# The second 512 columns of four output projections by Strassen's scheme, and the order of the adds behind the experts

## The chip, the cores and the metric

One core of a Trainium2 chip runs the whole program in one launch. The metric is the time on the device in microseconds (us); lower is better. The kernel before takes 2987.09 us, the median of 3 runs from 2985.12 to 2989.6.

TensorE (PE) multiplies and transposes. It reads SBUF and writes PSUM, which has 8 banks, each 512 float32 values wide on each of 128 partitions. VectorE (DVE), ScalarE (ACT) and GpSimd (POOL) do the rest; SyncE (SP) issues most DMAs. The engines run side by side and meet only at semaphores.

## The reference

Two blocks run one after the other on x, which is 512 tokens by 1024 features in float32. The first block has two layers, each a mixer and then a layer of 32 experts. The second block has two layers of this form, and all of it is float32:

```
u = rms_norm(h, mix_pre_g)                       # layer 0 dilated, layer 1 differential attention
y = attention(u, w_in, positions) @ w_out        # output projection 1 and 3
h = h + rms_norm(y, mix_post_g)
u = rms_norm(h, mem_pre_g)
y = memory_cross_attention(u, mem, wq, wkv) @ wo # output projection 2 and 4
h = h + rms_norm(y, mem_post_g)
u = rms_norm(h, ffn_pre_g)
h = h + rms_norm((silu(u @ w_gate) * (u @ w_up)) @ w_down, ffn_post_g)
```

An output projection is a 512x1024 by 1024x1024 product. The norm behind it needs a whole row of y, so both halves of the columns.

## The kernel before

**Data.** x stays in SBUF as four tiles of 128 tokens (`x_res`). The input of every projection lies transposed in `ring_feat` (`featv`, eight chunks of 128 features by 512 tokens). Weights come in pieces of 1024x512 through two ring slots, also part of `ring_feat`. A piece is loaded as soon as the piece two before it has been used.

**Output projections** (`out_projection`, line 2634). Half 0 makes columns 0 to 511, half 1 columns 512 to 1023. Each half takes the four token tiles in turn. A tile is eight products of 128x128 by 128x512, one for each chunk of features; each float32 product stands in the trace as two records. ACT squares a bank (L2609), DVE multiplies the same bank by the gain (L2613). After the second half of a tile, POOL takes the root of the mean square (L309, L311), DVE adds the scaled y to x (L2595), ACT squares and scales x for the next norm (L316, L324), with another root on POOL between them. PE transposes the scaled tile (L334) and DVE copies it to `featv` with the gain (L341). This runs one tile behind the products: tiles 0, 1 and 2 are transposed inside half 1, tile 3 inside the next stage. That stage is `memory_queries` (L2677) or `gate_up` (L2987). Each begins with four products of tokens 0 to 255 alone, and finishes them for tokens 256 to 511.

In three of the four projections PE begins half 0 early, while the attention still runs (`out_begin`, `out_products`, L2630). The differential attention leaves one of eight chunks for the end, the memory attention two. Only the dilated attention leaves all of them.

**Strassen's scheme** is already used for the query, gate, mix and down projections. The four blocks of each factor give seven block products in place of eight (Winograd's form). DVE forms four sums and four differences of blocks, each of 128x1024 (L2389 to L2404), before the products that read them. A group of seven products covers two token tiles of a 512-column piece. ACT then copies three products out of PSUM, DVE adds four times, POOL three times. In `down_projection` the last slot makes two such groups. Its outputs go through `down_outputs`, whose order of work is written by hand for each engine, and a layer's last tiles enter the next layer's norm from there.

**Behind the experts** (`combine`, `entry_norm`). For each token tile DVE adds two rows that were read back from DRAM (L1842, L1846). ACT squares tile 0, POOL takes its root, and ACT scales it only after it has squared tile 1. DVE waits for the root of tile 0 (`n_root`) before it adds tile 1. POOL also makes one spare power, at L1826, when the last expert rows have been stored.

Of the kernel before, what the change touches and what calls it, by code (L numbers as in the profile page):

```python
# [5 lines left out]
P = 128  # L6
D = 1024
S = 512
TT = S // P
# [67 lines left out]
def program(nc, a):  # L77
# [5 lines left out]
    with ctx:  # L83
# [265 lines left out]
        def entry_norm(name, eng, buf, gain, added=None, add=None):  # L349
# [3 lines left out]
            if name == "dve" and add:  # L353
                add(0)
                eng.wait_ge(n_root, j + 1)
# [5 lines left out]
            for t in range(TT):  # L361
# [8 lines left out]
                if name == "pool":  # L370
                    root_x(eng, j + t)
# [1436 lines left out]
        def spilled(name, eng, l):  # L1808
# [13 lines left out]
            if name == "pool":  # L1822
# [3 lines left out]
                G.tensor_tensor(out=stat[:, 254:255], in0=c_("ones")[:, 0:1], in1=stat[:, 255:256], op=ALU.pow)  # L1826
# [534 lines left out]
        STAGES = ("mix", "query", "gate", "down")  # L2361
        FAST = {"mix": 10, "query": 2, "gate": FC - 2, "down": 4}
        UP_FULL, SILU = {k: 7 for k in STAGES}, {"mix": 3, "query": 3, "gate": 5, "down": 5}
        HIDDEN, ADDED = {"mix": 4, "query": 4, "gate": 6, "down": 4}, {k: 3 for k in STAGES}
        SUMS = {"mix": 6, "query": 2, "gate": FC // 2, "down": DOWN_SLOTS}
# [268 lines left out]
        def out_projection(name, eng, l, post, nxt, attended=False):  # L2634

            buf = view(big, 0 if attended else 8192, TT, D)
# [6 lines left out]
            for half in range(2):  # L2643
                going = bool(begun) and half == 0
                if name != "pe" or not going:
                    n = take(name, "ring")
                    w = ring_slot(n, KC, 512)
                    if name == "pe":
                        eng.wait_ge(w_loaded[n % 2], 16 * (n // 2 + 1))
                for t in range(TT):  # L2650
                    if name == "pe" and going:
                        out_products(eng, t, range(begun["next"][t], KC)).then_inc(bank_full, 1)
                        take(name, "full")
                    elif name == "pe":
                        def job(bank, t=t, w=w):
                            for k in range(KC):
                                yield T.matmul(bank, featv[:, k, t * P:(t + 1) * P], w[:, k, :], start=k == 0, stop=k == KC - 1)  # L2657
                        pe_bank(eng, job, "both")
                        if half:
                            y_squares.append((bank_read_act, total["act"]))  # L2660
# [1001 lines left out]
```

## Time and profile before

| | us |
|---|---|
| median of 3 runs | 2987.09 |
| the profiled execution, its own time | 2987.54 |
| its span, first to last instruction | 2985.7 |
| PE busy | 2830.2 (95%) |
| DVE busy | 1122.7 (38%) |
| ACT busy | 662.0 (22%) |
| POOL busy | 516.5 (17%) |

The mean granted clock of TensorE over the span is 0.984 of full speed. The records of half 1 and the transposes around it are from 1511.7 to 1541.9 us (dilated), 1660.3 to 1690.4 (memory, layer 0), 2392.8 to 2422.9 (differential) and 2542.1 to 2572.2 (memory, layer 1). The adds behind the experts start at 598.13 us and at 1197.75 us.

The views used are the page itself, the timeline (start, duration, engine, line, operation, output and inputs, shape, count, and in brackets the idle time of the engine before it and what ended it), the view of one tile's instructions, and the view by stretches of time.

### The profile page before, as it was taken

How to read it: one execution, taken by the hardware profiler on the slowest of the kernel's cores; microseconds unless marked ns; L12 is line 12 of the kernel's file. 1: busy time of each engine (PE TensorE's matmuls, PEld its weight loads, DVE VectorE, ACT ScalarE, POOL GpSimd, SP SyncE). 2: the span in 40 equal slices, each digit the busy share in tenths (PEclk: the TensorE clock that was granted, in tenths of full speed). 3: DMA queues.
4: the chain of work that ended last, by engine and by line, in shares of the span. 5: the costliest groups of instructions: out<-in, count | busy, mean ns of one | idle time of the engine just before them, and what ended most of it. 6: DMA issues, size and time to landing. Idle time of an engine off the chain costs nothing.

```text
span 2985.7 us, 32062 instructions
## 1 busy us (share of the span) xinstructions
PE 2830.2 (95%) x12340; PEld 1902.8 (64%) x12340; DVE 1122.7 (38%) x2302; ACT 662.0 (22%) x1512; POOL 516.5 (17%) x799
## 2 busy tenths in 40 slices
PE   8999998789999988899999999999998999999998
PEld 4565543245655432586566688888685565688887
DVE  4543311145433110435532333344447632343354
ACT  3333110033331100104512211101205522211100
POOL 3111111131011111113300012201114510122201
PEclk9999999999999998999999999999999999999999
DMA  3106699831066999421011122222220030222222
GB/s 137 68 29 254 255 414 419 356 124 74 29 254 247 413 419 363 180 86 56 29 57 57 57 85 86 97 79 92 85 85 29 1 113 29 85 85 85 71 80 90
DMA packets 126415, 422.07 MB, mean 141 GB/s; under 512 B 10480, under 2 KB 14704, under 8 KB 103088
## 3 DMA queue, kind: packets, MB, share of 16 engines
q1 hardware_dynamic: 112944, 387.01, 34.0%
q0 software_dynamic: 12736, 30.84, 2.8%
q8 instruction: 101, 1.65, 0.2%
q10 hardware_dynamic: 576, 2.10, 0.2%
q14 instruction: 58, 0.48, 0.1%
HBM read 408.63 MB, written 27.26 MB: 146 GB/s over the span
## 4 chain that ended last, share of the span: by engine, by line
PE 74%; issue 9%; DMA 9%; DVE 3%; ACT 2%; POOL 1%; POOLq 1%; SPq 0%; DVEq 0%; ACTq 0%
PE ps L2424 34%; PE ps L417 7%; PE ps L2657 5%; PE ps L1643 5%; PE ps L1098 4%; DMA ring_feat<-in_w 3%; PE ps L2630 3%; PE ps L1684 2%; DMA big<-in_w 2%; PE ps L2531 2%; PE ps L2677 2%; PE ps L2987 2%; DMA rows<-in_w 2%; PE ps L1927 1%; PE ps L1914 1%
## 5 line engine op out<-in xcount | busy, mean ns | idle before, releaser
L417 PE MATMUL ps<-ring_feat 128*128 128x512 f32 (+2 forms) x704 | 277.3, 549 | 5.3 <-DVE ring_feat L341 2.7
L2424 PE MATMUL ps<-ring_feat 128*128 128x256 f32 x1216 | 276.9, 379 | 0.8 <-ACT big L285 0.8
L2424 PE MATMUL ps<-big 128*128 128x256 f32 x1200 | 268.1, 379 | 0.0
L2424 PEld LDWEIGHTS ps<-ring_feat 128*128 128x128 f32 x1216 | 231.0, 190 | 33.4 <-issue 2.1
L2424 PEld LDWEIGHTS ps<-big 128*128 128x128 f32 x1200 | 228.0, 190 | 31.0
L417 PEld LDWEIGHTS ps<-ring_feat 128*128 128x128 f32 x704 | 133.7, 193 | 132.7 <-issue 95.1
L2657 PE MATMUL ps<-ring_feat 128*128 128x512 f32 x320 | 139.4, 592 | 0.7 <-ACT ring_feat L2011 0.7
L1659 DVE TENSOR_TENSOR tmp<-tmp,ps 128x256 f32<-128x256 f32 x32 | 13.5, 421 | 306.1 <-ACT tmp L1653 306.1
L2424 PE MATMUL ps<-tmp 128*128 128x256 f32 x576 | 128.2, 379 | 0.0
L2424 PE MATMUL ps<-ring_feat,tmp 128*128 128x256 f32 x544 | 126.5, 379 | 0.0
L2424 PEld LDWEIGHTS ps<-tmp 128*128 128x128 f32 x576 | 109.4, 190 | 14.9
L1098 PE MATMUL ps<-ring_feat 128*128 128x512 f32 x256 | 113.3, 594 | 0.0
L2424 PEld LDWEIGHTS ps<-ring_feat,tmp 128*128 128x128 f32 x544 | 103.3, 190 | 14.1
L1643 PE MATMUL ps<-ring_feat,tmp 128*64 128x512 f32 x384 | 92.8, 632 | 19.5 <-DMA ring_feat<-in_w 15.1
L1643 PE MATMUL ps<-big,tmp 128*64 128x512 f32 x384 | 89.9, 614 | 22.3 <-DMA big<-in_w 17.3
L1698 POOL DMA_INDIRECT expert_out<-tmp,route_i x32 | 32.2, 1005 | 440.7 <-ACT tmp L1693 374.5
L2657 PEld LDWEIGHTS ps<-ring_feat 128*128 128x128 f32 x320 | 60.1, 190 | 73.4 <-issue 72.2
L2424 PE MATMUL ps<-ring_feat,big 128*128 128x256 f32 x400 | 95.5, 379 | 0.0
L2613 DVE TENSOR_TENSOR big<-ps,par 128x512 f32<-128x512 f32 x32 | 22.1, 691 | 179.2 <-ACT big L2609 179.2
L2630 PE MATMUL ps<-ring_feat 128*128 128x512 f32 x192 | 85.2, 595 | 4.1 <-ACT ring_feat L2249 2.3
L1653 ACT ACTIVATE tmp<-ps 128x256 f32<-128x256 f32 x32 | 12.3, 383 | 332.9 <-PE ps L1643 332.9
L1629 DVE TENSOR_TENSOR tmp<-ps,par 128x512 f32<-128x512 f32 x64 | 41.2, 686 | 113.0 <-PE ps L1620 113.0
(489 smaller groups left out, 4715.9 us busy)
## 6 DMA issues: line engine op xcount, KB each, us to landing
big<-in_w SPq DMA_DIRECT2D x36, 2048.0 KB, 22.1
ring_feat<-in_w SPq DMA_DIRECT2D x36, 2048.0 KB, 25.4
ring_feat<-in_w_gate_up SPq DMA_DIRECT2D x22, 2048.0 KB, 8.0
ring_feat<-in_w_mix_in SPq DMA_DIRECT2D x12, 2048.0 KB, 8.2
ring_feat<-in_w_down SPq DMA_DIRECT2D x12, 1536.0 KB, 6.7
par<-in_w SPq DMA_DIRECT2D x12, 1024.0 KB, 17.8
e_spare<-in_w SPq DMA_DIRECT2D x12, 1024.0 KB, 19.2
tmp<-in_w_mem_kv SPq DMA_DIRECT2D x6, 2048.0 KB, 27.4
```

Source lines behind the costliest of these rows:

```text
L417: yield T.matmul(bank, lhs(k), rhs(k), start=k == 0, stop=k == n - 1)
L1098: m = T.matmul(bank, featv[:, k, t * P:(t + 1) * P], w[:, k, :], start=k == 6, stop=k == 2)
L1629: m = V.tensor_tensor(e_xT[p % 2][:, 4 * b:4 * b + 4, :], ps[:, b, :].rearrange("p (k s) -> p k s", k=4), g[:, 4 * b:4 * b + 4].unsqueeze( ...
L1643: m = T.matmul(ps[h, u, :], e_xT[s][:, k, h], e_half(l, c, i)[k % 4], start=k == 0, stop=k == KC - 1)
L1684: m = T.matmul(ps[h, 6 + half, :], e_hT[:, k, h], e_half(l, c, i)[2 * k + half], start=k == 0, stop=k == 1)
L1698: eng.indirect_dma_start(out=a["expert_out"], out_offset=bass.IndirectOffsetOnAxis(ap=slots_out[:, p:p + 1], axis=0), in_=e_y[s], in_offse ...
L2424: m = T.matmul(to, lhs[:, j, :], rhs[:, j, :], start=start and j == 0, stop=stop and j == chunks - 1)
L2531: yield T.matmul(bank, featv[:, k, t * P:(t + 1) * P], w[:, k, :], start=k == 0, stop=k == KC - 1)
L2630: m = T.matmul(begun["banks"][t], featv[:, k, t * P:(t + 1) * P], begun["w"][:, k, :], start=k == 0, stop=k == KC - 1)
L2657: yield T.matmul(bank, featv[:, k, t * P:(t + 1) * P], w[:, k, :], start=k == 0, stop=k == KC - 1)
L2677: m = T.matmul(bank[:, tokens], w[:, k, (f % 4) * P:(f % 4 + 1) * P], featv[:, k, tokens], start=k == 0, stop=k == KC - 1)
L2987: m = T.matmul(bank[:, tokens], w[:, kk, o:o + P], featv[:, kk, tokens], start=kk == 0, stop=kk == KC - 1)
```

## The change

Half 1 of `out_projection` becomes two groups of seven block products (`out_group`): group 0 gives tiles 0 and 1, group 1 tiles 2 and 3. DVE forms the eight sums and differences (`sum_blocks`) in half 0, right after its read of tile 0. `down_outputs` becomes `block_outputs`, which all five such places share. PE transposes tiles 0 and 1 inside group 1, after its fifth and its sixth product. Tiles 2 and 3 are transposed in the next stage, behind three of its four first products; before, tile 3 alone was there, behind two.

Behind the experts, DVE no longer waits for the root of tile 0. The spare power at the end of `spilled` goes. In its place POOL makes one addition and one power, in the order of a root, just before it waits for the first square.

```diff
+        def ready_root(pool):
+            spot = stat[:, 254:255]
+            G.tensor_scalar(spot, c_("ones")[:, 0:1], EPS, None, ALU.add)
+            pool.drain()
+            G.tensor_tensor(out=spot, in0=spot, in1=stat[:, 255:256], op=ALU.pow)
...
             if name == "dve" and add:
                 add(0)
-                eng.wait_ge(n_root, j + 1)
                 add(1)
...
+                    if add and t == 0:
+                        ready_root(eng)
                     root_x(eng, j + t)
...
-                G.tensor_tensor(out=stat[:, 254:255], in0=c_("ones")[:, 0:1], in1=stat[:, 255:256], op=ALU.pow)
...
+                elif name != "pool":
+                    read_y(name, eng, y0 + t, t, 0, buf, gain)
+                if name == "dve" and t == 0:
+                    sum_blocks(eng, n + 1)
...
+                out_group(eng, stage, l, 0, w, out_sets[stage, l][0], ())
...
+                def turn(t):
+                    if t == 0:
+                        eng.wait_ge(hidden_ready, g_dve(stage, l, 0, D_C21))
+                    turn_x(name, eng, t)
+                out_group(eng, stage, l, 1, w, out_sets[stage, l][1], (lambda: turn(0), lambda: turn(1)))
+                feat_ready(eng, 1)
...
+        def sum_blocks(dve, n):
+            dve.drain()
+            form_sums(dve, *out_blocks(), [v.rearrange("p k (g n) -> p k g n", g=2) for v in out_feat_sum])
+            dve.wait_ge(w_loaded[n % 2], 16 * (n // 2 + 1))
+            differences(dve, ring_slot(n, KC, 512), out_w_diff)
...
+        def out_group(pe, stage, l, g, w, four, steps):
...
+            block_product(first[0], a11, lo[:, :, LO])
+            block_product(second[0], a12, hi[:, :, LO]).then_inc(up_full, 1)
+            if g == 0:
+                pe.wait_ge(blocks_summed, g_sums(stage, l, 0))
+            block_product(first[1], s2, t2).then_inc(up_full, 1)
+            block_product(first[2], s3, t3)
+            block_product(second[2], s1, t1).then_inc(up_full, 1)
+            if g:
+                steps[0]()
+            block_product(first[3], a22, t4)
+            if g:
+                steps[1]()
+            block_product(second[3], s4, hi[:, :, HI]).then_inc(bank_full if g else up_full, 1)
...
-                if i == 1:
+                if i == 2:
+                    turn_x(name, eng, TT - 2)
+                    if name == "pe":
+                        eng.wait_ge(hidden_ready, g_dve("attn", l, 1, D_C21))
                     turn_x(name, eng, TT - 1)
...
                 if half:
                     entry(0, x_turn)
+                if half and stage != "down":
+                    entry(1, x_turn)
                 corners(1)
```

In the listings of the order, a row is a line of the kernel, the operation, output and inputs, the shape and the count of instructions in a row; the changed kernel's lines are 7 higher around here. PE, the differential attention's projection, half 1 and the start of the queries, before (L2657 is half 1, L334 the transposes, L2677 the queries):

```order
L2657 MATMUL ps<-ring_feat 128x512 x16
L334 MATMUL ps<-cst,big 128x128 x8
L2657 MATMUL ps<-ring_feat 128x512 x8
L334 MATMUL ps<-cst,big 128x128 x8
L2657 MATMUL ps<-ring_feat 128x512 x8
L334 MATMUL ps<-cst,big 128x128 x8
L2677 MATMUL ps<-ring_feat 128x256 x16
L334 MATMUL ps<-cst,big 128x128 x8
L2677 MATMUL ps<-ring_feat 128x256 x48
```

The same place in the changed kernel (L2431 are the block products, L341 the transposes, L2747 the queries):

```order
L2431 MATMUL ps<-ring_feat 128x256 x8
L2431 MATMUL ps<-tmp 128x256 x12
L2431 MATMUL ps<-tmp,ring_feat 128x256 x4
L2431 MATMUL ps<-ring_feat,tmp 128x256 x4
L2431 MATMUL ps<-ring_feat 128x256 x8
L2431 MATMUL ps<-tmp 128x256 x12
L341 MATMUL ps<-cst,big 128x128 x8
L2431 MATMUL ps<-tmp,ring_feat 128x256 x4
L341 MATMUL ps<-cst,big 128x128 x8
L2431 MATMUL ps<-ring_feat,tmp 128x256 x4
L2747 MATMUL ps<-ring_feat 128x256 x24
L341 MATMUL ps<-cst,big 128x128 x16
```

32 products of 512 columns have become 56 of 256, and the transposes of tiles 0 and 1 stand before the last and the last but one block product. DVE at the same place, before (L2613 reads a bank, L2595 adds to x, L341 copies a transposed tile):

```order
L2613 TENSOR_TENSOR big<-ps,par 128x512 x5
L2595 SCALAR_TENSOR_TENSOR x_res<-big,nstat,x_res 128x1024
L2613 TENSOR_TENSOR big<-ps,par 128x512
L2595 SCALAR_TENSOR_TENSOR x_res<-big,nstat,x_res 128x1024
L341 TENSOR_TENSOR ring_feat<-ps,par 128x4x128 x2
```

And now, from its read of tile 0 in half 0 (L2620) on:

```order
L2620 TENSOR_TENSOR big<-ps,par 128x512
L2406 TENSOR_TENSOR tmp<-ring_feat 128x1024
L2407 TENSOR_TENSOR tmp<-ring_feat 128x1024
L2409 TENSOR_TENSOR tmp<-tmp,ring_feat 128x1024
L2411 TENSOR_TENSOR tmp<-ring_feat,tmp 128x1024
L2396 TENSOR_TENSOR tmp<-ring_feat 128x1024
L2397 TENSOR_TENSOR tmp<-ring_feat 128x1024
L2399 TENSOR_TENSOR tmp<-ring_feat,tmp 128x1024
L2401 TENSOR_TENSOR tmp<-ring_feat,tmp 128x1024
L2620 TENSOR_TENSOR big<-ps,par 128x512 x3
```

Eight operations of 128x1024 stand between the reads of tile 0 and tile 1. ACT in the changed kernel, from the copies of group 0 on (L3219 copies the plain product, L3224 and L3225 the outer ones, L3239 squares y, L316 squares x, L331 scales it):

```order
L3219 ACTIVATE tmp<-ps 128x256
L3224 ACTIVATE tmp<-ps 128x256
L3225 ACTIVATE tmp<-ps 128x256
L3239 ACTIVATE tmp,nstat<-big 128x512 x2
L3219 ACTIVATE tmp<-ps 128x256
L316 ACTIVATE big,nstat<-x_res 128x1024
L3224 ACTIVATE tmp<-ps 128x256
L3225 ACTIVATE tmp<-ps 128x256
L331 ACTIVATE big<-x_res,nstat 128x1024
L316 ACTIVATE big,nstat<-x_res 128x1024
L331 ACTIVATE big<-x_res,nstat 128x1024
```

The scaling of tile 0 stands behind the two outer copies of group 1.

## Rows read from the trace of the kernel before

**Rows 1.** The page: busy time by engine, and the chain that ended last.
```profile
PE 2830.2 (95%) x12340; PEld 1902.8 (64%) x12340; DVE 1122.7 (38%) x2302; ACT 662.0 (22%) x1512; POOL 516.5 (17%) x799
PE 74%; issue 9%; DMA 9%; DVE 3%; ACT 2%; POOL 1%; POOLq 1%; SPq 0%; DVEq 0%; ACTq 0%
```

**Rows 2.** Timeline (start, us, engine, line, ..., [idle before]), PE, differential's projection.
```profile
2392.78 13.90 PE L2657 MATMUL ps<-ring_feat 128*128 128x512 f32 x32
2406.51 1.04 PE L334 MATMUL ps<-cst,big 128*128 128x128 f32 x8
2407.39 7.03 PE L2657 MATMUL ps<-ring_feat 128*128 128x512 f32 x16
2414.26 1.04 PE L334 MATMUL ps<-cst,big 128*128 128x128 f32 x8
```

**Rows 3.** Timeline, PE, block products of the gate projection, layer 1.
```profile
2640.45 5.34 PE L2424 MATMUL ps<-big 128*128 128x256 f32 x24
2645.63 1.89 PE L2424 MATMUL ps<-big,ring_feat 128*128 128x256 f32 x8
```

**Rows 4.** Timeline, DVE: first of eight block sums, and what follows the last.
```profile
1551.25 1.23 DVE L2389 TENSOR_TENSOR tmp<-ring_feat 128x1024 f32<-128x1024 f32 x1
...
1561.00 0.68 DVE L288 TENSOR_SCALAR big<-ps 128x512 f32<-128x512 f32 x1
```

**Rows 5.** Timeline, DVE, first read of half 0, differential's projection.
```profile
2391.12 0.69 DVE L2613 TENSOR_TENSOR big<-ps,par 128x512 f32<-128x512 f32 x1 [14.48 <-ACT big L2609]
```

**Rows 6.** Timeline, the same read, then PE's half 1, memory projection, layer 0.
```profile
1656.11 0.69 DVE L2613 TENSOR_TENSOR big<-ps,par 128x512 f32<-128x512 f32 x1 [26.59 <-ACT big L2609]
...
1660.34 13.90 PE L2657 MATMUL ps<-ring_feat 128*128 128x512 f32 x32
```

**Rows 7.** Timeline, PE, end of layer 0's down projection, group 1 and two transposes.
```profile
2084.56 2.75 PE L2424 MATMUL ps<-ring_feat,tmp 128*128 128x256 f32 x12
...
2093.69 1.07 PE L334 MATMUL ps<-cst,big 128*128 128x128 f32 x8
2096.90 1.75 PE L334 MATMUL ps<-cst,big 128*128 128x128 f32 x8 [2.14 <-ACT big L324]
2098.44 14.97 PE L2531 MATMUL ps<-ring_feat 128*128 128x512 f32 x32
```

**Rows 8.** Timeline, ACT, the same place.
```profile
2091.24 0.38 ACT L3147 ACTIVATE cst<-ps 128x256 f32<-128x256 f32 x1 [1.19 <-PE ps L2424]
2092.39 1.15 ACT L324 ACTIVATE big<-x_res,nstat 128x1024 f32<-128x1024 f32 x1 [0.50 <-POOL nstat L311]
2095.69 1.15 ACT L324 ACTIVATE big<-x_res,nstat 128x1024 f32<-128x1024 f32 x1 [1.11 <-POOL nstat L311]
...
2104.98 2.30 ACT L324 ACTIVATE big<-x_res,nstat 128x1024 f32<-128x1024 f32 x2
```

**Rows 9.** Timeline, POOL and DVE side by side, the same place.
```profile
2087.64 1.91 POOL L309 TENSOR_SCALAR nstat<-nstat 128x1 f32<-128x1 f32 x1
...
2087.58 1.28 DVE L3221 SCALAR_TENSOR_TENSOR x_res<-big,nstat,x_res 128x1024 f32<-128x1024 f32 x1 [0.91 <-POOL nstat L311]
```

**Rows 10.** By stretches: us, PE busy (instructions), granted clock, DMA share, GB/s.
```profile
2093.80:2097.20 3.40, 1.26 (x11) 1.00 0.58 161
2097.20:2100.60 3.40, 3.40 (x11) 0.50 1.02 393
```

**Rows 11.** Timeline, DVE, POOL, ACT, then PE, behind layer 0's experts.
```profile
603.79 1.28 DVE L1842 SCALAR_TENSOR_TENSOR x_res<-big,stat,x_res 128x1024 f32<-128x1024 f32 x1 [3.01 <-POOL nstat L311]
...
603.19 0.57 POOL L311 TENSOR_TENSOR nstat<-nstat,stat 128x1 f32<-128x1 f32 x1 [0.75 <-issue]
...
607.53 1.13 ACT L324 ACTIVATE tmp<-x_res,nstat 128x1024 f32<-128x1024 f32 x1
...
608.80 1.94 PE L334 MATMUL ps<-cst,tmp 128*128 128x128 f32 x8 [6.53 <-ACT tmp L324]
```

**Rows 12.** View of the tile big, SP: the second load of tile 1 alone.
```profile
L1838 SPq DMA_DIRECT2D big<-expert_out x1: 432/432/432, 595.7 to 595.7; - x1
...
DMA to landing us min/median/max: 7.3/7.3/7.3
```

More of the change, by code:

```diff
@@ L2642, in out_projection @@
                 eng.wait_ge(l_out_read, KC)
[L2643 to L2660, printed above, removed]
-                    elif name != "pool":
-                        read_y(name, eng, y0 + t, t, half, buf, gain)
-                    if half:
-                        add_tile(name, eng, y0 + t, j0 + t, t, buf, nxt)
-                        late[name] = (j0, buf, p2(l, nxt))
-                        if t >= 1:
-                            turn_x(name, eng, t - 1)
-                slot_done(name)
-                begun.clear()
@@ new lines, in out_projection, with job @@
+            going = bool(begun)
+            if name != "pe" or not going:
+                n = take(name, "ring")
+                w = ring_slot(n, KC, 512)
+                if name == "pe":
+                    eng.wait_ge(w_loaded[n % 2], 16 * (n // 2 + 1))
+            for t in range(TT):
+                if name == "pe" and going:
+                    out_products(eng, t, range(begun["next"][t], KC)).then_inc(bank_full, 1)
+                    take(name, "full")
+                elif name == "pe":
+                    def job(bank, t=t, w=w):
+                        for k in range(KC):
+                            yield T.matmul(bank, featv[:, k, t * P:(t + 1) * P], w[:, k, :], start=k == 0, stop=k == KC - 1)
+                    pe_bank(eng, job, "both")
+                elif name != "pool":
+                    read_y(name, eng, y0 + t, t, 0, buf, gain)
+                if name == "dve" and t == 0:
+                    sum_blocks(eng, n + 1)
@@ new lines, in out_projection @@
+            end = take(name, "full")
+            if name != "pe":
+                block_outputs(name, eng, stage, l, 0, 1, out_sets[stage, l], end, buf, gain, y0, j0, p2(l, nxt), out_staged, out_junk)
+            if name in ("act", "pool"):
+                turn_x(name, eng, 0)
+                turn_x(name, eng, 1)
+            slot_done(name)
+        out_sets = {}
+        out_feat_sum = [view(tmp, i * 1024, KC // 2, 256) for i in range(4)]
+        out_w_diff = [view(tmp, 4096 + i * 1024, KC // 2, 256) for i in range(4)]
@@ L3126, in down_group, with block_outputs @@
                 m4.then_inc(up_full, 1)
-        def down_outputs(name, eng, l, half, sets, end, buf, post, y0, j0, nxt):
+        def block_outputs(name, eng, stage, l, unit0, half, sets, end, buf, post, y0, j0, nxt, staged, junk):
             cols = slice(half * 512, (half + 1) * 512)
@@ L3150, in square @@
             def square(g):
-                n = 2 * half + g
+                n = unit0 + g
                 for i in range(2):
@@ L3182, in gain @@
             def gain(t):
-                eng.wait_ge(silu_ready, g_act("down", l, 2 * half + t // 2, D_SQUARE + t % 2))
+                eng.wait_ge(silu_ready, g_act(stage, l, unit0 + t // 2, D_SQUARE + t % 2))
                 V.tensor_tensor(buf[:, t, cols], buf[:, t, cols], post[:, cols], ALU.mult)
```

96 lines of the change are left out of this document (65 added, 31 removed).

## Prediction

> **What bounds the kernel now.** I read the page first: PE is busy for 95% of the span, and three quarters of the chain that ended last is PE [rows 1]. So a microsecond of PE's work that goes is worth a microsecond, and a microsecond in which PE waits costs one. The timeline of PE around the four output projections came next. In half 1 PE has no gap: a tile's 16 records take 2414.26 - 2407.39 = 6.87 us, and a transposed tile 2407.39 - 2406.51 = 0.87 us [rows 2]. Whatever the change makes PE wait for there is a new wait, not a longer old one. Then the timelines of DVE, ACT and POOL at the same places, and at the one place where a Strassen group already hands its tiles to a norm, the end of layer 0's down projection. It shows what the new chain costs.
>
> **Products.** Before, half 1 is 4 x 6.87 = 27.5 us. A block product of 8 records takes (2645.63 - 2640.45) / 3 = 1.727 us [rows 3], so 14 of them take 24.2 us. PE gains 3.3 us a projection, 13.2 us in all four. The transposes are as many as before.
>
> **The wait for the block sums.** DVE forms eight blocks of 128x1024, which take 1561.00 - 1551.25 = 9.75 us with what lies between them [rows 4]. It may start only behind its read of half 0's first tile, and PE needs the result for the third product of group 0, 2 x 1.727 = 3.45 us into it.
> - Differential: DVE's read ends at 2391.12 + 0.69 = 2391.8 [rows 5], the sums at 2401.6. PE has finished half 0 at 2392.78 [rows 2], because seven of its eight chunks were made during the attention, and comes to the third product at 2396.2. It waits 5.4 us.
> - Memory, both layers: the read ends at 1656.8, the sums at 1666.6; PE comes at 1660.34 + 3.45 = 1663.8 [rows 6]. It waits 2.8 us, twice. Layer 1 has the same distances.
> - Dilated: half 0 takes its full 27.5 us, and the sums end some 6.9 + 1.7 + 9.8 = 18 us into it. No wait. This cover is what the other three lack.
>
> Sum: 5.4 + 5.6 = 11.0 us. The reads of tiles 1 to 3, now queued behind the sums on DVE, are late by 10 us, but PE needs their banks only in group 1, 8.6 us after the wait has ended.
>
> **The wait for tile 0.** PE turns tile 0 after five products of group 1, which is 5 x 1.727 = 8.6 us after group 0's end. ACT scales that tile only behind its two outer copies, and these read the fifth product. In the down projection the same copies start 0.2 us after the fifth product (a group there is (2093.69 - 2084.56) / 7 = 1.30 us a product, so the fifth ended at 2091.1) [rows 7, 8]. Two copies at a distance of 0.3 and a length of 0.4 make 0.7, the scaling 1.15, the semaphore 0.1: PE waits 2.1 us. The rest of the chain, from group 0's end to the scaling, took 2092.39 - 2084.56 = 7.8 us there [rows 7, 8]; here the copies end after 9.5, so it is hidden.
>
> **The wait for tile 1.** Its scaling started 2095.69 - 2092.39 = 3.3 us after tile 0's, and PE's transposes 4.5 us after that of tile 0, at 2096.90 [rows 7, 8]. POOL's outer additions and the root lie in between, and the change leaves them so. Here that is 0.9 + 4.5 = 5.4 us after the fifth product; PE has used 2.1 + 0.9 + 1.7 = 4.7 us. It waits 0.7 us. Both together are 2.8 us a projection and 11.2 us in all: nearly what the products give back.
>
> **Tiles 2 and 3.** PE turns them behind three first products of the next stage, 3 x 3.45 = 10.4 us after group 1, and 11.3 us. In the down projection their scaling ended at 2104.98 + 2.30 = 2107.3, 13.6 us after the group [rows 7, 8], but DVE had there first to copy two turned tiles; the change puts both copies ahead. I take off 2.4 us for the corners that start that much earlier and 1.3 us for the second copy, which gives 9.9 us: no wait, with little to spare. The DVE sums of the next stage come some 4 us later; PE needs them 17 us after its last turn, so they are covered.
>
> **The clock.** In the down projection PE waited 2.14 us. The stretch with that wait was 1.26 of 3.40 us busy, and in the next the granted clock was 0.50, which is 1.2 GHz in place of 2.4 [rows 10]. The transposes took 1.75 us in place of 1.07 and the 32 records behind them 14.97 in place of 13.90 [rows 2, 7]: 1.7 us lost. The change brings seven waits of 2.1 us or more (one of 5.4, two of 2.8, four of 2.1). The rows have one of this length and it lost the clock. Bounds: none, or eight losses (the long one twice), so 0 to 13.6 us. I take four, the middle, since one case is all that I have for waits of 2.1 us, and the longer ones are surer: 6.8 us. Behind a wait for tile 0, the slower product hides the wait for tile 1; two such take 1.4 off: 5.4 us.
>
> **Behind the experts.** DVE added tile 1 at 603.79, when the root had come; ACT scaled tile 0 at 607.53 [rows 11], 3.7 us later, and 2.4 after DVE's second operation on the tile. Without the hold that second operation waits for the row's other half, which landed at 595.7 + 7.3 = 603.0 [rows 12], so ACT can scale at about 605.5. Everything behind shifts with it: 2.0 us. The second place is alike; 4.0 us for both. Bounds: nothing, if the root is later than ACT's second square by as much as is won, and 3.0 us each, the time that DVE was held [rows 11]. The spare root should turn the 0.75 us before the power into 0.2 [rows 11]; that root has then half a microsecond to spare before ACT has squared tile 1, so I cost it at nothing, and 0.6 us a place if it fails and is late.
>
> DVE's additions overlap POOL's root now. An addition of y to x from 2087.58 to 2088.86 kept a POOL instruction on a single column busy for 1.91 us, past its own end [rows 9], so the root may end only behind DVE's second operation, at 604.4, plus 0.6 to 1.0 us: 605.0 to 605.4, just in time. The Trainium skill has this as a rule: in SBUF — State Buffer, section Who interferes with whom, a DVE instruction with two SBUF inputs blocks a GpSimd one that reads SBUF, fully. By that rule both steps of the root could stand behind the addition and take most of the gain. The trace agrees that the block is whole.
>
> **Sum**, against the profiled execution's own time of 2987.54 us: -13.2 products, +11.0 block sums, +11.2 tiles 0 and 1, +5.4 clock, -4.0 experts: +10.4, 2997.9 us. The median of the runs is 0.45 us below that execution, so **2997.5 us**. A difference of 0.2% (6.0 us) is about what a measurement can tell here.
>
> **The rivals.**
> - *The clock holds.* At most one loss of 1.7 us. 2987.1 + 5.0 to + 6.7: 2992.1 to 2993.8. For it: in all of the kernel before, a granted clock of 0.984 leaves few losses, though PE often waits in its attention. Against: the row of 2.14 us. 15%.
> - *The clock goes almost every time.* Seven or eight losses less the hidden waits: 5.0 + 13.6 - 2.8 = +15.8 on 2987.1: 3002.9. 10%.
> - *Tiles 2 and 3 are late.* If their chain keeps the 13.6 us of the down projection, PE waits 2.3 us in each next stage: +9.2, so 3006.7. Against: DVE's order there. It decides where ACT's last scaling ends more than 11.3 us after group 1. 8%.
> - *The root is held up behind the experts.* Both of its steps wait for both additions, and the hold was worth as much as it cost: 4.0 us back, 3001.5. 8%.
> - *Faster: the block sums are in time.* At DVE, in the three projections begun early: if the eight operations ended before PE's third product, 11.0 us and the longest idle stretches went, and with them the clock losses: 2987.1 - 13.2 + 11.2 - 4.0 = 2981.1. It decides at 4.4 us for the eight in the differential projection, and 7.0 in the memory ones; against it stand 9.75 us [rows 4] and DVE's order, in which nothing of them is ahead of the read. 5%.
>
> **How the numbers follow.** My forecast, two to six clock losses, has 54% and reaches from 2994 to 3001. Slower by over 0.2% is above 2993.1: the forecast, three slower rivals and a third of the first, 85% less a little for what I have not seen: 0.82. Faster: 0.05. Between: 0.13. Range for 8 in 10: 2990 to 3005.
>
> **What would show it.** In the trace of the changed kernel: block products at 1.727 us; in the differential projection an idle gap of PE of about 5.4 us before the third product, released by DVE's last block sum, and 2.8 us in both memory projections, none in the dilated one; before the transposes of tile 0 a gap of 2.1 us and of tile 1 one of 0.7 us, both released by ACT's scaling, four times; no gap at tiles 2 and 3; the transposes of tile 0 behind the experts with an idle time of about 4.5 us in place of 6.53; a lower granted clock right behind some four of the long gaps. I am wrong if the gaps for the block sums are missing or PE reaches the third product later than I say, if ACT scales tile 0 before the fifth product, or if the clock holds throughout.

## The result

The changed kernel takes **2999.96 us**, the median of 6 runs (2999.51 to 3006.94), beside 2988.28 us for the kernel before (6 runs, 2985.12 to 2989.6). It is slower: the medians differ by 11.7 us, the means by 13.8. The ratio over all runs, which is not that of the two medians, is 1.0046, with a 95% interval from 1.0035 to 1.0056, or 10.5 to 16.7 us. The forecast was 2997.5 us, in a range from 2990 to 3005. The profiled execution took 3004.23 us, 16.7 more than that of before, with a granted clock of 0.982 in place of 0.984.

The page first: PE's busy time and the chain of the changed kernel, then the group of its block products whose operands lie in `tmp`, then, from the view that groups PE's instructions by line and tile (busy time, mean ns, idle time before and its releaser), its transposes out of `big`:

```profile
PE 2828.3 (94%) x12532; PEld 1944.1 (65%) x12532; DVE 1172.0 (39%) x2366; ACT 669.7 (22%) x1536; POOL 561.8 (19%) x825
PE 72%; issue 9%; DMA 8%; DVE 4%; ACT 2%; POOL 2%; SPq 1%; POOLq 1%; DVEq 1%; ACTq 0%
...
L2431 PE MATMUL ps<-tmp 128*128 128x256 f32 x768 | 177.4, 389 | 11.1 <-DVE tmp L2401 11.1
L341 PE MATMUL ps<-cst,big 128*128 128x128 f32 x160 | 21.1, 282 | 12.6 <-ACT big L331 12.6
```

PE has only 1.9 us less to do than in [rows 1], although products worth 13 us are gone: more of the rest runs at half the clock. Part of that lies behind the experts, since experiment 1, which leaves the projections as they were, has PE busy for 2835.0 us. Against that the changed kernel has 6.7 us less: 13.2 of products, and 6.4 given back in the projections (below). Beside that stand two new idle times. 11.1 us are waits for DVE's last block sum. 12.6 us are waits for ACT's scaling, where before had the 2.14 us of the down projection alone [rows 7]; so 10.4 us are new. They are called turn waits below, since PE turns (transposes) a tile behind each.

The timeline of PE shows the whole pattern in the differential attention's projection (start, duration, ..., [idle before]). It answers to [rows 2]:

```profile
2396.85 3.62 PE L2431 MATMUL ps<-ring_feat 128*128 128x256 f32 x16
2405.87 8.14 PE L2431 MATMUL ps<-tmp 128*128 128x256 f32 x24 [5.40 <-DVE tmp L2401]
...
2415.57 1.89 PE L2431 MATMUL ps<-ring_feat,tmp 128*128 128x256 f32 x8
2417.30 3.62 PE L2431 MATMUL ps<-ring_feat 128*128 128x256 f32 x16
2420.75 5.34 PE L2431 MATMUL ps<-tmp 128*128 128x256 f32 x24
2427.97 1.06 PE L341 MATMUL ps<-cst,big 128*128 128x128 f32 x8 [1.87 <-ACT big L331]
2428.87 1.89 PE L2431 MATMUL ps<-tmp,ring_feat 128*128 128x256 f32 x8
2431.49 1.09 PE L341 MATMUL ps<-cst,big 128*128 128x128 f32 x8 [0.73 <-ACT big L331]
...
2434.15 10.52 PE L2747 MATMUL ps<-ring_feat 128*128 128x256 f32 x48
2444.51 1.91 PE L341 MATMUL ps<-cst,big 128*128 128x128 f32 x16
```

Two products need nothing from DVE. Then PE stands for 5.40 us. The next three products take 8.14 us; the same three of group 1 take 5.34. Those 2.80 us are the clock, as the view by stretches shows (length, PE busy, PEld, DVE, ACT, POOL, granted clock, DMA share, GB/s):

```profile
2401.10:2404.50 3.40, 0.00 (x0) 0.00 (x0) 3.33 (x3) 0.00 (x0) 0.00 (x0) 1.00 1.05 398
2404.50:2407.90 3.40, 2.03 (x5) 1.67 (x6) 3.33 (x6) 0.00 (x0) 0.00 (x0) 0.50 0.37 139
2407.90:2411.40 3.50, 3.50 (x10) 2.78 (x9) 0.46 (x2) 0.00 (x0) 0.00 (x0) 0.51 0.00 0
```

PE did nothing in the first stretch, and the clock granted in the second and third was 0.50, which is 1.2 GHz. Tiles 2 and 3 cost no wait: their 16 transposes at 2444.51 follow the queries' products without a gap. The memory projections show the same with waits of 2.83 and 2.82 us, and one stretch at 0.50 behind each, where the three products take 7.13 us; in the dilated one the third product follows at once:

```profile
1665.98 7.13 PE L2431 MATMUL ps<-tmp 128*128 128x256 f32 x24 [2.83 <-DVE tmp L2401]
...
2560.75 7.13 PE L2431 MATMUL ps<-tmp 128*128 128x256 f32 x24 [2.82 <-DVE tmp L2401]
...
1514.72 5.34 PE L2431 MATMUL ps<-tmp 128*128 128x256 f32 x24
```

**The sum by stages**, each from the first record of half 1 to the next stage's first block product (start times from PE's timeline):

| projection | before | changed | difference |
|---|---|---|---|
| dilated | 58.68 | 58.31 | -0.4 |
| memory, layer 0 | 58.60 | 63.09 | +4.5 |
| differential | 59.54 | 67.62 | +8.1 |
| memory, layer 1 | 58.59 | 63.09 | +4.5 |

They add up to 16.7 us, the difference of the two profiled executions. Everything ahead of 1484 us gave 0.5 us. Some 0.5 was lost again outside the four stages, 0.4 of it between layer 0's memory projection and the differential one; what took it is not shown.

### The profile page after: what moved, and what is told of

Read it like the earlier page. It is cut to its first block, busy times and chain, and to the rows that moved or that the text cites. A ratio compares the mean times of both kernels' runs of the same rounds, so it can differ in the third digit from the quotient of the medians.

```text
span 3002.4 us, 32609 instructions
## 1 busy us (share of the span) xinstructions
PE 2828.3 (94%) x12532; PEld 1944.1 (65%) x12532; DVE 1172.0 (39%) x2366; ACT 669.7 (22%) x1536; POOL 561.8 (19%) x825
## 4 chain that ended last, share of the span: by engine, by line
PE 72%; issue 9%; DMA 8%; DVE 4%; ACT 2%; POOL 2%; SPq 1%; POOLq 1%; DVEq 1%; ACTq 0%
PE ps L2431 37%; PE ps L425 7%; PE ps L1651 5%; PE ps L1106 4%; DMA rows<-in_w 2%; PE ps L2637 2%; DMA big<-in_w 2%; PE ps L1692 2%; DMA ring_feat<-in_w 2%; PE ps L2538 2%; PE ps L2747 2%; PE ps L3060 2%; PE ps L1910 1%; PE ps L1934 1%; PE ps L1921 1%
## 5 line engine op out<-in xcount | busy, mean ns | idle before, releaser
L2431 PE MATMUL ps<-ring_feat 128*128 128x256 f32 x1344 | 305.8, 379 | 0.8 <-ACT big L285 0.8
L2431 PEld LDWEIGHTS ps<-ring_feat 128*128 128x128 f32 x1344 | 255.3, 190 | 38.4 <-issue 4.0
L2431 PE MATMUL ps<-big 128*128 128x256 f32 x1200 | 268.1, 379 | 0.0
L2431 PEld LDWEIGHTS ps<-big 128*128 128x128 f32 x1200 | 228.0, 190 | 31.0
L425 PEld LDWEIGHTS ps<-ring_feat 128*128 128x128 f32 x704 | 134.2, 193 | 133.2 <-issue 95.7
L2431 PE MATMUL ps<-tmp 128*128 128x256 f32 x768 | 177.4, 389 | 11.1 <-DVE tmp L2401 11.1
L2431 PEld LDWEIGHTS ps<-tmp 128*128 128x128 f32 x768 | 149.9, 196 | 33.8 <-DVE tmp L2401 12.3
L2431 PE MATMUL ps<-ring_feat,tmp 128*128 128x256 f32 x608 | 141.7, 379 | 0.0
L2431 PEld LDWEIGHTS ps<-ring_feat,tmp 128*128 128x128 f32 x608 | 115.1, 190 | 15.6
L1106 PE MATMUL ps<-ring_feat 128*128 128x512 f32 x256 | 113.3, 594 | 0.0
L1651 PE MATMUL ps<-ring_feat,tmp 128*64 128x512 f32 x384 | 92.4, 631 | 19.1 <-DMA ring_feat<-in_w 14.7
L2431 PE MATMUL ps<-ring_feat,big 128*128 128x256 f32 x400 | 95.5, 379 | 0.0
L2637 PE MATMUL ps<-ring_feat 128*128 128x512 f32 x192 | 85.2, 595 | 4.1 <-ACT ring_feat L2256 2.3
L2431 PEld LDWEIGHTS ps<-ring_feat,big 128*128 128x128 f32 x400 | 76.0, 190 | 10.3
L1106 PEld LDWEIGHTS ps<-ring_feat 128*128 128x128 f32 x256 | 47.2, 190 | 52.6 <-issue 52.6
L1651 PEld LDWEIGHTS ps<-big,tmp 128*64 128x64 f32 x384 | 27.8, 143 | 79.6 <-issue 57.8
```

Of the source, the lines that this page charges most:

```text
L425: yield T.matmul(bank, lhs(k), rhs(k), start=k == 0, stop=k == n - 1)
L1106: m = T.matmul(bank, featv[:, k, t * P:(t + 1) * P], w[:, k, :], start=k == 6, stop=k == 2)
L1651: m = T.matmul(ps[h, u, :], e_xT[s][:, k, h], e_half(l, c, i)[k % 4], start=k == 0, stop=k == KC - 1)
L2431: m = T.matmul(to, lhs[:, j, :], rhs[:, j, :], start=start and j == 0, stop=stop and j == chunks - 1)
L2637: m = T.matmul(begun["banks"][t], featv[:, k, t * P:(t + 1) * P], begun["w"][:, k, :], start=k == 0, stop=k == KC - 1)
```

## The experiments

Two theories were to be told apart in each case. The first: the loss is DVE's block sums and ScalarE's order of work, each a separate wait, and the clock follows the long waits. Its rival: the waits only moved time that Strassen's scheme costs anyway, or the low clock was chance in one execution. The first four kernels ran on one chip beside 31 runs of before (2989.0 us), the last four on one chip beside 27 (2988.16 us). Ratios are to these, over all runs and not of the two medians.

| kernel | median us | lowest to highest | ratio, 95% interval |
|---|---|---|---|
| 1. experts' part alone | 2985.86 | 2983.55 to 2988.01 | 0.9989 [0.9979, 0.9998] |
| 3. copies of a product in the wait | 2996.13 | 2993.55 to 3000.03 | 1.0022 [1.0012, 1.0032] |
| 4. early differences | 2985.96 | 2981.68 to 2990.14 | 0.9987 [0.9977, 0.9996] |
| 5. ScalarE's other order | 2995.98 | 2991.91 to 2998.87 | 1.0021 [1.0012, 1.0031] |
| 2. no hold, spare root as before | 2985.36 | 2982.39 to 2988.13 | 0.9988 [0.9979, 0.9997] |
| 6. Strassen in the dilated projection alone | 2984.93 | 2981.6 to 2988.81 | 0.9985 [0.9976, 0.9994] |
| 7. early differences and other order | 2980.74 | 2976.95 to 2985.22 | 0.9973 [0.9964, 0.9982] |
| 8. the changed kernel again | 3002.64 | 2999.7 to 3003.7 | 1.0045 [1.0031, 1.0058] |

**1. The experts' part alone.** The projections are those of before.

```diff
                 add(0)
-                eng.wait_ge(n_root, j + 1)
                 add(1)
...
+                    if add and t == 0:
+                        ready_root(eng)
                     root_x(eng, j + t)
```

> The kernel before with the part behind the experts alone: no hold on tile one's addition, spare root first. Theory A (the half-rate stretch eats it): PE's first transposes behind the experts start 1.6 us earlier, reckoned from the first read-back, but the granted clock comes back at the same time as before, so PE's next work is slower for longer and only 0.5 to 0.6 us a place are left; 1.1 us in all, about 2987.2. Theory B (my forecast's term): the 2.0 us a place pass through, 4 us in all, about 2984.3. Rival C: the root is late behind DVE's additions, and the transposes start no earlier; no change.

Measured: 3.1 us less than before, with an interval from 0.6 to 6.3. Theory A's 1.1 and theory B's 4 both lie in it. VectorE's add of tile 1, PE's first transposes behind it and the last ones, in the first place (first three rows) and the second, answer to [rows 11]:

```profile
600.79 1.28 DVE L1849 SCALAR_TENSOR_TENSOR x_res<-big,stat,x_res 128x1024 f32<-128x1024 f32 x1 [0.94 <-DMA big<-expert_out]
605.80 1.94 PE L341 MATMUL ps<-cst,tmp 128*128 128x128 f32 x8 [4.29 <-ACT tmp L331]
625.97 1.04 PE L341 MATMUL ps<-cst,tmp 128*128 128x128 f32 x8
...
1204.09 1.28 DVE L1849 SCALAR_TENSOR_TENSOR x_res<-big,stat,x_res 128x1024 f32<-128x1024 f32 x1 [1.45 <-DMA big<-expert_out]
1209.10 1.94 PE L341 MATMUL ps<-cst,tmp 128*128 128x128 f32 x8 [4.58 <-ACT tmp L331]
1230.29 1.04 PE L341 MATMUL ps<-cst,tmp 128*128 128x128 f32 x8
```

The transposes start 5.01 us after that add, as before (608.80 - 603.79). What went is the hold: DVE's idle time fell from 3.01 us to 0.94, and now a DMA ends it. In the second place it fell from 2.86 us to 1.45. How much comes off depends on when tile 1's expert rows land, which differs from run to run: in the changed kernel's first place the idle time was 1.44 us, and in experiments 3 and 4, which have no hold either, a DMA kept VectorE idle for 2.95 and 2.87 us there.

Theory A's point, that products at half the clock eat part of the gain, can be read too. The last transposes stand in the kernel before as follows, and there the clock is whole in every profile (1.04 us for 8 records, where the first ones take 1.94):

```profile
628.03 1.04 PE L334 MATMUL ps<-cst,tmp 128*128 128x128 f32 x8
...
1230.42 1.04 PE L334 MATMUL ps<-cst,tmp 128*128 128x128 f32 x8
```

From VectorE's first add behind the experts to these, in us:

| | first place | second place | less than before |
|---|---|---|---|
| before (adds at 598.13, 1197.75) | 29.90 | 32.67 | |
| experiment 1 (597.19, 1199.99) | 28.78 | 30.30 | 1.1 + 2.4 = 3.5 |
| experiment 2 (601.00, 1200.13) | 29.05 | 30.51 | 0.9 + 2.2 = 3.0 |
| changed kernel (597.75, 1198.56) | 29.39 | 31.38 | 0.5 + 1.3 = 1.8 |

In the first place theory A was right: the transposes came 2.06 us earlier after the first add (8.61 in place of 10.67), and 1.12 us was left behind the slow products. In the second place it went the other way: the transposes came 1.42 us earlier and 2.37 us was left, since the products behind took 8.55 us in place of 9.51.

**2. The hold without the spare root.** Only the wait goes; the spare power stays at the end of `spilled`.

> The kernel before, with one edit behind the experts: VectorE no longer waits for GpSimd's root before it adds to tile two; the spare root stands where it stood. The output projections are untouched. Theory A (the hold is what cost): ScalarE scales tile one only after it has squared tile two, so the 0.75 us before the first root lies beside the add of tile two; the transposes behind the experts come as early as with both edits, about 5.0 us behind the start of that add, and the time is that of the run with the experts' part alone, 2985.9 us, give or take 1.2. Theory B (the spare root is what gained): without it the first root is late by its 0.75 us and holds the scale of tile one, the transposes come 0.7 us later than with both edits in each of the two places, and the time is 2987.3 us. Theory C (the hold protected the root from VectorE's adds): the root beside the adds takes over 1.5 us, and the time is 2989 us or more.

Measured: 2985.36 us, 2.8 us below before, like the run with both edits (3.1). The times can't tell theory A from theory B, which lie 1.4 us apart; the trace can. GpSimd's root of tile 0, VectorE's adds beside it and ScalarE's scaling:

```profile
605.08 0.93 POOL L307 TENSOR_SCALAR nstat<-nstat 128x1 f32<-128x1 f32 x1 [7.08 <-ACT tmp L316]
606.76 0.95 POOL L311 TENSOR_TENSOR nstat<-nstat,stat 128x1 f32<-128x1 f32 x1 [0.75 <-issue]
...
604.64 1.28 DVE L1841 SCALAR_TENSOR_TENSOR x_res<-big,stat,x_res 128x1024 f32<-128x1024 f32 x1 [0.98 <-DMA big<-expert_out]
606.00 1.28 DVE L1845 SCALAR_TENSOR_TENSOR x_res<-big,stat,x_res 128x1024 f32<-128x1024 f32 x1
...
608.37 1.13 ACT L324 ACTIVATE tmp<-x_res,nstat 128x1024 f32<-128x1024 f32 x1
609.65 1.94 PE L334 MATMUL ps<-cst,tmp 128*128 128x128 f32 x8 [4.14 <-ACT tmp L324]
```

The two steps of the root take 0.93 and 0.95 us beside VectorE's adds, where in the kernel before, with VectorE held, the power took 0.57 [rows 11]; each ends 0.1 to 0.4 us behind the end of an add. By the Trainium skill, SBUF — State Buffer, section Who interferes with whom, a VectorE instruction with both inputs in SBUF, when it has started first, keeps a GpSimd one that reads SBUF out for its whole length; the trace agrees. Even with the 0.75 us before the power the root is done at 607.71. ScalarE comes to the scaling at 608.37, since it squares tile 1 first. The transposes again start 5.01 us after the add of tile 1 (609.65 - 604.64), as theory A said. So the hold is all of the gain. The spare root's new place cuts the 0.75 us before the power to 0.47 in experiment 1, which is worth nothing here.

**3. The clock by itself.** While PE would wait for the block sums it repeats its first block product, which is started again from zero afterwards. The sums are as late as ever, but PE is not idle.

```diff
             if g == 0:
+                for chunks in {("attn", 1): (4, 4, 4), ("mem", 0): (4, 2), ("mem", 1): (4, 2)}.get((stage, l), ()):
+                    block_product(first[1], a11, lo[:, :, LO], chunks)
                 pe.wait_ge(blocks_summed, g_sums(stage, l, 0))
             block_product(first[1], s2, t2).then_inc(up_full, 1)
```

> The changed kernel, with products that nobody reads ahead of PE's wait for the block sums: three block products (5.2 us) in the differential projection, one and a half (2.6 us) in each memory projection. They are written over by the third product. Theory: the wait for the sums keeps its end, the idle time there shrinks from 5.4 to 0.2 us and from 2.8 to 0.2 us, and the four half-rate stretches behind these waits are gone: 4 x 1.7 = 6.8 us less than the changed kernel, about 2993. Rival: the clock falls at these places for another reason than PE's idleness, and the time stays at 3000.

Measured: 2996.13 us, which is 7.1 over the kernel before, where the changed kernel was 11.7 and 14.5 over: 4.6 to 7.4 us less, with 6.8 expected. PE's timeline in the differential projection, and two stretches of it:

```profile
2394.68 8.80 PE L2431 MATMUL ps<-ring_feat 128*128 128x256 f32 x40
2403.70 5.45 PE L2431 MATMUL ps<-tmp 128*128 128x256 f32 x24 [0.22 <-DVE tmp L2401]
...
2398.30:2401.70 3.40, 3.40 (x17) 2.99 (x17) 3.33 (x4) 0.38 (x1) 0.00 (x0) 1.00 1.02 389
2405.10:2408.50 3.40, 3.40 (x17) 3.01 (x16) 1.05 (x3) 0.00 (x0) 0.00 (x0) 1.00 0.00 0
```

The third product starts 9.02 us after the first, as in the changed kernel (2405.87 - 2396.85), but it and the next two take 5.45 us in place of 8.14, and the clock is whole. The stage takes 64.93 us in place of 67.62, the memory ones 61.42 in place of 63.09: 6.0 us for the three. So the low clock behind these waits comes from PE's idleness and is not a second cost of the products that follow.

**4. The block sums in time.** The four weight differences are formed before half 0's products are read, into memory that is free there; only the four sums of features stay behind the first read.

```diff
-        out_w_diff = [view(tmp, 4096 + i * 1024, KC // 2, 256) for i in range(4)]
+        out_w_diff = [view(e_spare, i * 1024, KC // 2, 256) for i in range(3)] + [view(rows, 0, KC // 2, 256)]
...
+            if name == "dve":
+                early_differences(eng, n + 1)
             for t in range(TT):
```

> The changed kernel, with the four differences of weights made by DVE before its read of half 0's first tile, into buffers that are free there; the four sums of features stay behind that read. Theory: DVE's block sums are what PE waits for. They end 4.9 us earlier: the wait in the differential projection falls from 5.4 to 0.5 us, in the memory ones from 2.8 to nothing, and with the idle time the four half-rate stretches go: 10.5 + 6.8 = 17 us less than the changed kernel, about 2982.7, under the kernel before. Rival 1: the clock falls at the remaining waits of 1.9 us now, and 10.5 us are won: 2989.5. Rival 2: the early differences hold DVE while the attention still needs it, and give back some 5 us a projection.

Measured: 2985.96 us, 3.0 us below before, where 5.6 was expected, and 14.7 to 17.5 less than the changed kernel. The differential projection, where the longest wait was:

```profile
2393.10 3.62 PE L2431 MATMUL ps<-ring_feat 128*128 128x256 f32 x16
2397.24 5.45 PE L2431 MATMUL ps<-e_spare,tmp 128*128 128x256 f32 x24 [0.53 <-DVE tmp L2411]
...
2416.65 1.06 PE L341 MATMUL ps<-cst,big 128*128 128x128 f32 x8 [1.88 <-ACT big L331]
```

5.40 us have become 0.53, the waits of the memory projections are gone, and no stretch near a projection shows a clock of 0.50. The stages take 58.32 (memory, both) and 60.06 us: 4.8 us less for each memory projection and 7.6 for the differential one. Yet the kernel only equals the experts' part alone (2985.86). The turn waits are left, and they eat nearly all that the products give: the four stages together are 0.4 us shorter than before. Rival 1 is out, since no turn wait has a low clock behind it. Rival 2 is out too: in the differential projection the early differences run from 2377.09 to 2382.05 us, and DVE then idles for 9.40 us before its read of tile 0, where it had idled for 14.47.

**5. ScalarE's other order.** In half 1's second group ScalarE scales tile 0 before its outer copies, and GpSimd takes tile 1's root before its own outer additions.

```diff
                 if half:
                     entry(0, x_square)
+                if half and stage != "down":
+                    entry(0, x_scale)
                 copy_outer(1)
...
+                if half and stage != "down":
+                    entry(1, x_root)
                 outer(1)
```

> The changed kernel, with ACT's scaling of tile 0 ahead of its outer copies of group 1, and POOL's root of tile 1 ahead of its outer additions, in the four output projections. Theory: ACT's order makes the wait before the transposes of tile 0. It falls from 1.87 to 0.4 us; the wait before tile 1 grows from 0.73 to 1.5 us; tiles 2 and 3 are still in time: 0.7 us a projection, 2.8 us in all, about 2997. Rival: the chain from group 0 sets that wait, not ACT's order, and it stays near 1.9 us; or the outer additions, now later, make PE wait for tiles 2 and 3 by about 1 us each time, and nothing is won.

Measured: 2995.98 us, 7.0 over before, which is 4.7 to 7.5 less than the changed kernel; 2.8 was expected. The dilated projection: GpSimd's root of tile 0 and ScalarE in the changed kernel first, then ScalarE in this one:

```profile
1530.61 0.56 POOL L311 TENSOR_TENSOR nstat<-nstat,stat 128x1 f32<-128x1 f32 x1
...
1532.19 0.38 ACT L3224 ACTIVATE tmp<-ps 128x256 f32<-128x256 f32 x1 [3.34 <-PE ps L2431]
1532.47 0.38 ACT L3225 ACTIVATE tmp<-ps 128x256 f32<-128x256 f32 x1
1532.73 1.15 ACT L331 ACTIVATE big<-x_res,nstat 128x1024 f32<-128x1024 f32 x1
```
```profile
1529.76 1.15 ACT L331 ACTIVATE big<-x_res,nstat 128x1024 f32<-128x1024 f32 x1 [2.36 <-POOL nstat L311]
1530.81 0.37 ACT L3224 ACTIVATE tmp<-ps 128x256 f32<-128x256 f32 x1
```

In the changed kernel ScalarE idles for 3.34 us on PE's fifth product. The root of tile 0 has come at 1531.17, 1.0 us before ScalarE goes on, and the scaling stands behind the copies until 1532.73. In the other order the scaling waits for that root alone. PE's wait for tile 0 falls from 1.87 to 0.35 us, that for tile 1 rises only from 0.73 to 0.90 where 1.5 was expected, and a stage is 1.36 us shorter: 56.96 for the dilated one (1509.82 to 1566.78), 61.7 for the memory ones. ScalarE's and GpSimd's edits were not tried apart, so which of them set the 0.90 is open. The waits for the block sums are as they were, and so are the low clocks behind them, but for one: after the same 5.40 us of idleness the three products took 6.93 us here and 8.14 in the changed kernel, with one stretch at 0.50 in place of two.

```profile
2401.49 6.93 PE L2431 MATMUL ps<-tmp 128*128 128x256 f32 x24 [5.40 <-DVE tmp L2401]
```

**6. Strassen in the dilated projection alone.** Of the edit to the projections only this call is kept; the other three run as before.

```diff
+        def fast(stage, l):
+            return stage not in ("attn", "mem") or (stage, l) in (("attn", 0),)
...
+            if not fast(stage, l):
+                return plain_projection(name, eng, l, post, nxt, attended)
```

> The changed kernel with Strassen's scheme in the second half of the first (dilated) output projection alone; the other three projections compute those columns as before. Experts' part as changed. Theory A (block sums and clock are the loss): in the dilated projection the sums are ready in time, the stage from the start of those columns to the next stage's block products takes 58.3 us against 58.7 before, no stretch at 0.50 of the clock behind it, and the time is that of the experts' part alone less 0.4 us: 2985.5 us, give or take 1.2. Theory B (the turn waits of 1.9 and 0.7 us cost what Strassen saves, or more): 2986 to 2989 us, with over 59 us for the stage. No wait of over 1 us is left at the three other projections under either.

Measured: 2984.93 us, 3.2 us below before. The stage takes 58.32 us (1509.19 to 1567.51) against 58.68 before, with the turn waits and no other:

```profile
1512.65 5.34 PE L2435 MATMUL ps<-tmp 128*128 128x256 f32 x24
...
1531.95 1.06 PE L341 MATMUL ps<-cst,big 128*128 128x128 f32 x8 [1.88 <-ACT big L331]
...
1535.47 1.09 PE L341 MATMUL ps<-cst,big 128*128 128x128 f32 x8 [0.73 <-ACT big L331]
```

The timeline bears out theory A, and none of the other three projections has a wait of its own any more. The times can't tell it from no change, since 0.4 us is below what the runs resolve.

**7. Both repairs.** The edits of 4 and 5 together.

> The changed kernel with both repairs: the weight differences are formed ahead of the projection's first half (as in the run with early differences), and ScalarE scales tile one before it copies the second outer product (as in the run with the other order). Theory A (the waits are separate and add up): no wait before the third block product, the wait of 1.9 us before the first transposes falls to 0.35 us and that of 0.7 us rises to 0.9, 1.4 us less in each of four stages, so 57.0 us for the dilated, 57.0 for each memory stage; the time is that of early differences alone less 5.5 us: 2980.5 us. Theory B (the clock takes part of it: fewer and shorter waits save their length only where the clock is whole): 2982 to 2984 us. Theory C (the other order holds up what ScalarE has to do next): 2986 us or more.

Measured: 2980.74 us, 7.4 us faster than before (5.4 to 10.8) and 22 below the changed kernel on the same chip. PE in layer 0's memory projection:

```profile
1656.55 3.62 PE L2431 MATMUL ps<-ring_feat 128*128 128x256 f32 x16
1660.01 5.34 PE L2431 MATMUL ps<-e_spare,tmp 128*128 128x256 f32 x24
...
1677.76 1.06 PE L341 MATMUL ps<-cst,big 128*128 128x128 f32 x8 [0.33 <-ACT big L331]
...
1681.46 1.09 PE L341 MATMUL ps<-cst,big 128*128 128x128 f32 x8 [0.91 <-ACT big L331]
```

The stage takes 56.95 us against 58.60 before and 63.09 in the changed kernel; the dilated one takes 56.96, the differential 58.72, the other memory one 56.94. Together the four are 5.8 us shorter than before. That is theory A, which had 57.0 for three of them: the two repairs add up. The median lies within 0.3 us of theory A's; the times alone (2977.4 to 2982.8 by the interval) would not rule out the lower end of theory B.

**8. The changed kernel again.**

> The changed kernel itself, beside the others, so that its time and theirs come from one chip. Theory A (waits and clock as in its first profile): three waits for block sums of 2.8, 5.4 and 2.8 us, each with a stretch at 0.50 of the clock directly behind it, 63.1, 67.6 and 63.1 us for these stages; 3000 us, 14 above early differences. Theory B (the stretches were chance in that one execution): in a second profile at least one of the three waits has no stretch at 0.50 behind it.

Measured: 3002.64 us. The waits are 2.82, 5.39 and 2.82 us, the stages 63.0, 66.3 and 62.8 us, and behind each wait the clock was 0.50 once more:

```profile
1666.70:1670.10 3.40, 3.30 (x8) 2.65 (x9) 2.17 (x5) 0.00 (x0) 0.00 (x0) 0.50 0.34 125
2404.00:2407.40 3.40, 2.88 (x7) 2.34 (x8) 2.59 (x5) 0.00 (x0) 0.00 (x0) 0.50 0.19 68
2557.60:2561.00 3.40, 2.91 (x7) 2.38 (x8) 2.55 (x5) 0.00 (x0) 0.00 (x0) 0.50 0.48 178
```

The low clock is no chance of one execution. Behind the 5.39 us it held for one such stretch this time, where the first profile had two; so this stage took 66.3 us and not the 67.6 of theory A.

## Why the prediction was right, step by step

The forecast of 10.4 us over before stands beside 11.7 in the first call (10.5 to 16.7 by its interval) and 14.5 in the second (9.3 to 17.3). Sign, cause and place were right; the size was somewhat low.

The forecast counted products at their distance from start to start, 1.727 us. The idle times of the profile are counted from the end of a record, and a record's end overlaps the next one's start by 0.16 us (1.89 - 1.727). A wait costs PE that overlap too. In the forecast's own count the terms are:

| term | forecast | measured in the first profile |
|---|---|---|
| products | -13.2 | -13.2 |
| block sums | +11.0 | +11.5: 11.05 of gaps, three overlaps |
| turn waits, tiles 0 and 1 | +11.2 | +11.7: 10.4 of gaps, eight overlaps |
| clock | +5.4 | +6.4 |
| the four stages | +14.4 | +16.4; the stages themselves, +16.7 |
| experts | -4.0 | -1.8 at the two places |

- **Products: right.** Block products are 1.727 us apart (2415.57 to 2417.30).
- **Block sums: right.** 5.40, 2.83, 2.82 and none. DVE's order behind its read, and the half 0 that PE had made ahead, were read rightly from [rows 4 to 6]. Experiment 4 takes most of these waits away and the clock losses with them.
- **Tile 0, 2.1 each: right.** The gap is 1.87, with the overlap 2.03. ScalarE scales behind its outer copies, and those wait for the fifth product; experiment 5 shows both.
- **Tile 1, 0.7 each: a little low.** The gap is 0.73, with the overlap 0.89.
- **Tiles 2 and 3, nothing: right**, in all four.
- **Clock, +5.4: near in size, and partly by luck.** Four was the middle of the forecast's bounds, and there were four stretches at 0.50 in the first profile. But all four stood behind the waits for the sums, which the forecast called the surer ones: 1.79, 2.80 and 1.79 us, 6.4 in all. None came behind the eight turn waits, to which it gave some of them, so the 1.4 us taken off for hidden waits had nothing to stand on. One row at 2.14 us was too little to price a wait of 1.87.
- **Experts, -4.0: the shift was read rightly, what follows from it was not.** ScalarE scaled tile 0 at 605.59, where the forecast had about 605.5. But "everything behind shifts with it" did not hold: the products behind ran at half the clock for longer, 8.74 us in place of 7.70 in the first place and 10.14 in place of 9.51 in the second. Of the shift, 0.5 and 1.3 us were left in the changed kernel.

By 1484 us the changed kernel was ahead by 0.5 us and not by 1.8. VectorE's first add in the second place starts when a DMA lands, anywhere from 1197.75 to 1201.27 us in the ten profiles, so one profile against another can't tell what passes through. The medians can a little: the four kernels without the hold and without the long waits (experiments 1, 2, 4 and 6) lie 2.8 to 3.2 us below before, and their projections give at most 0.4 of that. An estimate from these numbers is +16.7 for the stages and -3 for the experts, +14 in all. The means of the first call differ by 13.8 us, the medians by 11.7 and, in the second call, 14.5. Why the median of the first six runs is 4 us below their own profiled execution was not found; one stretch at 0.50 in place of two behind the longest wait, worth 1.2 us, may be a part of it.

The rival with the block sums in time was priced at 2981.1 us and given 5%, since nothing in the changed kernel made DVE faster. Experiment 4 built that case. It is 3.0 us below before, where the rival had 6.0. The rival's terms for the stages came to -2.0 us and the stages measured -0.4. The turn waits, 2.94 us with the overlaps in place of 2.8, and the 0.7 by which the differential projection's sums are still late (0.53 of gap and an overlap) make 1.3 of that difference. The rest of the shortfall lies outside the stages, where the experts' 4.0 had come to about 3; these runs can't resolve it further.

## What to carry to other kernels

Seven products in place of eight pay 3.3 us for these 512 columns, and an output projection with a norm behind it has little slack: look first for who forms the sums and whether the engine that multiplies arrives before them, above all where part of its work was already moved ahead. A wait of PE's costs its gap and 0.16 us of lost overlap; those of 2.14 us and more often had products at half the clock behind them as well. An engine that idles on the last product while another tile becomes ready has its order wrong: two reorderings turned a kernel 12 to 14 us slower into one 7 us faster, of which the hold behind the experts is about 3. A shift ahead of products at half the clock does not pass through whole.

## What the runs showed of the hardware

- All nine waits for block sums of 2.8 us or 5.4 us in the changed kernel (twice) and in experiment 5 had a granted clock of 0.50 behind them. None of the 17 waits of 1.87 or 1.88 us did, in the changed kernel (twice) and experiments 3, 4 and 6. The wait of 2.14 or 2.15 us at the end of layer 0's down projection, which is in all ten profiles, lost the clock in seven and kept it in three: in experiment 7 the transposes behind it took 1.09 us (below), in before 1.75 [rows 7].

```profile
2091.45 1.09 PE L341 MATMUL ps<-cst,big 128*128 128x128 f32 x8 [2.14 <-ACT big L331]
```

- After the same 5.4 us of idleness the three products behind took 6.83 and 6.93 us in two profiles, with one stretch at 0.50, and 8.14 us in a third, with two. At the whole clock they take 5.34.
- A product made for nothing was cheaper here than 2.8 or 5.4 us of idleness: experiment 3 has 48 more records than the changed kernel and takes 6.0 us less in the three stages.
